# Second attention: the copy of each output's high half moved from VectorE to ScalarE

## The reference

```
s_ctx = einsum(q, kc) * scale ;  s_win = where(valid, einsum(q, k) * scale, -inf)
p = softmax_with_sink(concat([s_ctx, s_win]), sink)
o = p[ctx] @ vc + p[win] @ v          # 16 heads
y = o @ w_o                           # the output projection
```

## Time and profile before

| what | us |
|---|---|
| three runs | 1575.88, 1576.94, 1579.33 (median 1576.94) |
| the profiled execution, its own time | 1575.75 |
| its span (first to last instruction) | 1574.0 |
| TensorE busy over the span | 1484.5 (94%) |
| VectorE busy over the span | 734.7 (47%) |
| ScalarE busy over the span | 598.3 (38%) |
| mean granted TensorE clock | 0.974 of full speed |

### The profile page before, as it was taken

One profiled execution on the slowest core, in us unless ns is written; L12 is line 12 of the kernel. 1 busy time (PEld: TensorE's weight loads), 2 busy tenths in 40 slices (PEclk: granted clock), 3 DMA queues, 4 the chain that ended last, 5 costly groups with the idle time before them and its releaser, 6 DMA issues.

```text
span 1574.0 us, 22641 instructions
## 1 busy us (share of the span) xinstructions
PE 1484.5 (94%) x9376; PEld 1251.6 (80%) x9376; DVE 734.7 (47%) x1204; ACT 598.3 (38%) x1130; POOL 277.4 (18%) x224
## 2 busy tenths in 40 slices
PE   7899999979999898999999998999999899999997
PEld 6878779847865586888888886688998678899997
DVE  6762145334349744323232234764454773255453
ACT  4434144244337625222122224442343461333342
POOL 2000187002000010211011111244500120021121
PEclk9899999899999998999999999999999999999999
DMA  7412464687200033313232232133351342646450
GB/s 230 164 55 85 160 245 139 252 332 279 81 27 1 28 107 143 125 58 139 85 107 74 95 120 112 54 108 107 114 192 44 107 162 107 267 171 211 168 174 28
DMA packets 36109, 206.84 MB, mean 131 GB/s; under 512 B 4952, under 2 KB 9480, under 8 KB 14888
## 3 DMA queue, kind: packets, MB, share of 16 engines
q1 hardware_dynamic: 33344, 200.11, 35.1%
q10 hardware_dynamic: 1848, 2.52, 0.8%
q0 software_dynamic: 816, 2.78, 0.5%
HBM read 202.76 MB, written 2.62 MB: 130 GB/s over the span
## 4 chain that ended last, share of the span: by engine, by line
PE 84%; DVE 7%; ACT 3%; DMA 3%; issue 1%; POOL 1%; SPq 1%; ACTq 0%; DVEq 0%; POOLq 0%
PE lin L1800 18%; PE lin L1802 17%; PE lin L1801 17%; PE lin L1767 4%; PE lin L1910 4%; PE lin L2381 4%; PE modp L1838 2%; DMA ring<-ada_in 2%; PE lin L2432 1%; PE lin L1783 1%; PE lin L1784 1%; PE lin L1785 1%; PE lin L2160 1%; PE aux L2302 1%; PE aux L1937 1%
## 5 line engine op out<-in xcount | busy, mean ns | idle before, releaser
L620 DVE TENSOR_TENSOR w_split<-ring,w_split 128x1024 fp32r<-128x1024 f32 (+1 forms) x140 | 187.5, 1344 | 358.7 <-ACT w_split L615 358.3
L615 ACT ACTIVATE w_split<-ring 128x1024 fp32r<-128x1024 f32 (+1 forms) x140 | 157.9, 1132 | 413.2 <-PE lin L1802 366.2
L1800 PE MATMUL lin<-hn_hi,w_split 128*128 128x512 f32 (+1 forms) x768 | 266.8, 347 | 3.5 <-DVE w_split L620 3.5
L1802 PE MATMUL lin<-hn_hi,w_split 128*128 128x512 f32 (+1 forms) x768 | 265.4, 346 | 0.0
L1801 PE MATMUL lin<-hn_lo,w_split 128*128 128x512 f32 (+1 forms) x728 | 249.9, 343 | 0.0
L1800 PEld LDWEIGHTS lin<-hn_hi,w_split 128*128 128x128 f32 x768 | 146.2, 190 | 21.1 <-issue 4.1
L1802 PEld LDWEIGHTS lin<-hn_hi,w_split 128*128 128x128 f32 x768 | 146.3, 190 | 17.5
L1801 PEld LDWEIGHTS lin<-hn_lo,w_split 128*128 128x128 f32 x728 | 138.7, 191 | 16.0 <-issue 0.5
L1801 PE MATMUL lin<-hid_split,w_split 128*128 128x512 f32 (+1 forms) x392 | 133.8, 341 | 0.0
L569 POOL TENSOR_TENSOR hn<-hn 128x256 f32<-128x256 f32 (+1 forms) x42 | 43.8, 1042 | 481.1 <-ACT hn L684 480.6
L1800 PE MATMUL lin<-hid_split,w_split 128*128 128x512 f32 (+1 forms) x352 | 118.5, 337 | 2.4 <-POOL hid_split L584 2.4
(11 more groups left out here) (435 smaller groups left out, 2978.7 us busy)
## 6 DMA issues: line engine op xcount, KB each, us to landing
ring<-ada_in SPq DMA_DIRECT2D x48, 1024.0 KB, 5.0
ring<-ssm_in_in SPq DMA_DIRECT2D x24, 1024.0 KB, 4.8
ring<-od_in_in SPq DMA_DIRECT2D x12, 1024.0 KB, 5.0
ring<-ffn0a_in_in SPq DMA_DIRECT2D x11, 1024.0 KB, 4.8
ring<-ffn0b_in_in SPq DMA_DIRECT2D x11, 1024.0 KB, 4.7
ring<-ffn1a_in_in SPq DMA_DIRECT2D x11, 1024.0 KB, 6.3
ring<-ffn1b_in_in SPq DMA_DIRECT2D x11, 1024.0 KB, 4.8
ring<-ev_in_in SPq DMA_DIRECT2D x9, 1024.0 KB, 13.6
```

The lines of the kernel that those rows point to most:

```text
L615: act.activation(parts[:, 0], w, ACT.Copy).then_inc(sig("w_high"), 1)
L620: dve.tensor_tensor(parts[:, 1], w, parts[:, 0].bitcast(F32), ALU.subtract).then_inc(sig("w_low"), 1)
L1800: mm(lin[0:m, tile % RING, 0:width], hi, x_hi, start=kt == 0, stop=False)
L1802: ins = mm(lin[0:m, tile % RING, 0:width], lo, x_hi, start=False, stop=kt == kts - 1)
```

## The change

A new function `out_high(i)` in ScalarE's list copies the bank with the outputs of pair i to `hn_hi` and counts the semaphore `out_high`. It stands behind the exponentials of (i, 1) and ahead of the two copies L800 that follow them, for pair i-2; for pair 7 it stands behind all of the attention's copies. VectorE's cast goes, and its subtraction waits for `out_high`. Everything else, TensorE's list too, stays as it was.

```diff
+            def out_high(i):
+                tile = output_tile(i)
+                full(act, "lin", tile)
+                act.activation(hn_hi[:, i, :], lin[:, tile % RING, :], ACT.Copy).then_inc(sig("out_high"), 1)
+
...
                 for j in range(3):
                     if i < AT_PAIRS:
                         exps(i, j)
+                    if j == 1 and i > 1:
+                        out_high(i - 2)
                     if i > 0 and j < 2:
                         turned_out(i - 1, j, (0, 1))
...
                 if 5 <= i < 8:
                     weights_hi(act, "w_o", i - 5)
+            out_high(AT_PAIRS - 1)
             full(act, "lin", turned_tile(AT_PAIRS - 1, 1, 2))
             weights_hi(act, "w_o", 3)
...
                 tile = output_tile(i)
                 full(dve, "lin", tile)
-                own.link(dve.tensor_copy(hn_hi[:, i, :], lin[:, tile % RING, :]))
+                dve.wait_ge(sig("out_high"), i + 1)
                 frees(tt(out_lo[:, i, :], lin[:, tile % RING, :], hn_hi[:, i, :].bitcast(F32), ALU.subtract), "lin", tile)
```

## The result

| | before | changed |
|---|---|---|
| median of 22 runs each | 1577.93 us (1572.82 to 1583.87) | 1582.09 us (1578.49 to 1588.15) |
| the profiled execution | 1575.75 us, span 1574.0 | 1581.15 us, span 1579.4 |

The account below looks back on a forecast made before the run. No engine fills a plain window; a chain through TensorE bounds it. Six windows lose 5.65 us, less 0.07 at the end: net 5.6, 1581.3 for the profiled execution, 1582.5 as median; range 1580.6 to 1584.5, whole range 1579.5 to 1585.5.

Parts of the forecast that it names:

- the mechanism: Second attention: ScalarE reaches the copy only after exponentials awaiting VectorE's L1109; subtraction, then L1100, wait; copy starts 1.5 us late.
- The distance from L1109 to L1100: Start to start in steps 2 to 7: 2.89 us, against old 1.41, 2.22 (steps 3 to 6) and 1.40.
- The hop: From the end of ScalarE's copy to the start of VectorE's subtraction: 0.04 us.
- The six windows: Second attention, between first L1100s: losses 1.48, 4 × 0.67 and 1.49, together 5.65 us; plain window 10.86.
- The bank: Subtraction frees it for each step's last transposes, 0.7 us later in plain steps; costed at nothing, uncovered 0.5 a step.
- The end: Behind pair 6's outputs, on the path to `w_o`: copy and hop 0.65 us against 0.72, 0.07 gained.
- Pair 7: Last pair's copy and delayed `w_o` weight work cost nothing, as TensorE comes over 8 us after the subtraction.
- granted clock 1.00 there: Expected TensorE clock in the changed kernel's second attention: 1.00 (2.4 GHz), with TensorE busy 9.5 of 10.86 us.
- The rival with the clock: Added TensorE idle lowers its clock to 0.68 for 10 us of work: 1587.2 us; chance 0.08 together with the bank rival.
- the forecast of 1581.3: Profiled execution's time after the change: 1575.75 plus net 5.6 us; on the runs' median scale 1582.5.
- The rule on offloading: Saturated VectorE's work may move to ScalarE; by it a gain, at most the faster rival's 4.4 us (chance 0.03).

Follow-up runs that it names:

- experiments two to six: Changed kernel, ratios to before: copy ahead of exponentials 0.9997; later 1.0079; unused ScalarE copy, VectorE casting 0.9996; pairs 1-4 only 1.0008; pairs 0, 5 only 1.0013.
- the last: Changed kernel with TensorE's scores (i, 2) ahead of the transposes of pair i-1's second head; ratio to before 1.0017, plain windows 10.89 us.
- second profile: The kernel before run again with no edit, for another profile; one execution, 1582.19 us, plain windows 10.19 us.
- the first experiment: The changed kernel again with no edit, timed against the kernel before; ratio 1.0027, median 1581.84 us.
- the late copy: Changed kernel with ScalarE's copy moved behind the two copies of transposed probabilities; ratio to before 1.0079, plain window 11.86 us.

## Why the prediction was right

1582.5 was predicted and 1582.09 measured, and the mechanism is the one predicted; experiments two to six and the last show it. That the two numbers are only 0.4 us apart is in part luck: the forecast was 5.6 us above a median of three runs, 1576.94, and over 22 runs the kernel before has 1577.93, so that the difference itself came out at 4.2. Term by term:

**The distance from L1109 to L1100** was put at 2.89 us and measured 2.93 to 2.94 in all six steps (501.15 to 504.08 in step 4). From L787 to the copy 1.44 (1.43 taken), the copy 0.59 (0.61 taken), from its end to the subtraction 0.10 where 0.04 was taken, and 0.61 from there to L1108 as taken. The hop was the mis-sized piece. My row for it, L615 to L620, gave 0.03 in all; here the chain between the copy and the subtraction has 0.03 and 0.04 of "issue" and 0.02 of VectorE's own sequencer at the wait's line:

```profile
503.38 0.03 issue
503.41 0.02 DVEq L1144
503.43 0.04 issue
```

The subtraction waits for two semaphores and L620 for one, which may be why; that was not tested.

**The six windows**: 5.65 predicted, 68.75 less 62.89 = 5.86 measured. The difference is the hop, 0.06 us longer six times, less the copy's 0.02 us. Plain 10.89 (10.86 predicted), the outer two 13.17 and 12.03 (13.1 and 12.0).

**The bank**: costed at nothing. TensorE does wait for the subtraction before the last transposes, 0.40 us in step 4, and 4.8 us in five times over the attention. It had room for it: 0.80 us of idle before the next transposes were left even so (1.20 us together, where the prediction has one wait of 1.36). The windows follow VectorE and ScalarE to 0.01 us without it.

```profile
504.31 0.63 PE L2153 MATMUL lin<-ident,arena 128*128 128x128 f32 x4 [0.40 <-DVE hid_split L1145]
```

**The end**: 0.07 us of gain was predicted behind pair 6's outputs. The copy began at 546.40 and the subtraction at 547.10, 0.70 against the old 0.73, so 0.03. Pair 7 was hidden as argued. But the stretch from the last L1108 to `w_o` was 0.79 us longer, against "granted clock 1.00 there", and this expectation was wrong. The clock went to its lower level, 1.2 GHz, for three microseconds:

```profile
541.00:544.00 3.00, 2.90 (x14) 2.09 (x15) 2.93 (x9) 3.00 (x9) 0.00 (x0) 0.50 0.22 27
```

I had read from the earlier trace rows that this much idle leaves the clock alone. The kernel before itself disproves it, in its second profile. The rival with the clock was wrong too, as it laid the price on the change: the price is real, but the kernel before pays it at times as well.

**The sum of the two profiles**: 5.86 + 0.79 = 6.65 us from the first L1100 of step 1 to `w_o`, less 1.25 us by which the changed execution reached that L1100 earlier (469.13 against 470.38), before anything that was changed. That is the 5.40 us by which the spans differ; behind `w_o`'s start both took 1031.1 us. So the forecast of 1581.3 for the profiled execution met 1581.15 partly by luck: two deviations that it did not foresee, 0.79 and 1.25 us, partly cancelled. Over 22 runs the medians are 4.2 us apart, below 5.6, though the interval of 3.3 to 6.0 holds it. One reason may be that in the changed kernel a stretch of low clock in window 2 (0.84 over the window) cost nothing, since TensorE had idle time there, while in window 1 of the kernel before it cost 1.38 us. That is argued from single profiles of different windows, not shown. The mean granted clocks of whole executions point the same way. In the session of the first experiment they average 0.9699 over 29 executions of the kernel before and 0.9712 over 12 of the changed one. A straight line of time against this clock, with one slope for both kernels (738 us for 1.00 of clock), puts the changed kernel 5.2 us (standard error 0.7) above the kernel before at the same clock, against 4.2 us between the two means. So a little more clock in the changed kernel's executions accounts for 1.0 of the missing 1.4 us; what gave it to them was not tested.

**The rule on offloading.** The Trainium skill (Perfetto Trace Analysis, Optimizing Scalar/DVE Operations) says that work may go to ScalarE if VectorE is saturated. With 9.17 of 10.19 us in a plain window it nearly was, and the same move of the same copies was worth 5.9 us lost or 1.0 us won in the six windows by where it stood in ScalarE's order. The rule is silent on the order.

## What to carry to other kernels

When a step moves to another engine, look first at what that engine's queue does ahead of it, and what that work waits for. Here the copy was put behind exponentials that wait for the very engine which then waits for the copy: two engines that had run side by side took turns. Moving it ahead of them removed the whole loss, and shortening the path through TensorE, which the chain of waits had named, brought more than relieving the busiest helper: 3.1 us in the four plain windows against 1.0 us in windows 1 and 6.

## What the runs showed of the hardware

The granted clock falls to 1.2 GHz for stretches of three to seven microseconds inside the second attention in ten of these twelve profiles, in kernels with and without more idle on TensorE, and two profiles of the same kernel before differ in it: none in the first, two in the second. What one cost differs. Ten profiles have one behind the last L1100, and there the way to `w_o` was longer than the 9.65 us of the first profile: by 0.5 to 1.7 us in nine of them, by 2.8 in the kernel with the late copy, whose stretch was the longest. In window 1 five had one; it cost 1.4 us at most, and twice nothing. In window 2 of the changed kernel it cost nothing; at full clock TensorE has 1.2 us of idle in such a window. A difference of a microsecond between two single profiles of this kernel is therefore no evidence unless the clock of that window is the same; the plain windows at full clock repeat to 0.02 us.
